# A two-layer decoder step: layer 0's prompt attention laid between its sample batches, with key transposes moved to VectorE

## The reference

```python
# layer 0, per sample request: 8 FoX heads of 64 and 4 differential heads of 2x64, one cache row of 1024 floats
k_all = concatenate([cache_k[pt].reshape(past, 1024), k_b]); v_all likewise; c = cumsum(logf)
sa = q . k * scale + (cq - ck)                  # FoX: causal softmax, then . v
pb = softmax(q . k * scale); diff = pb[0] - lam * pb[1]
ob = rms_norm(diff . v, subln0) * (1 - LAMBDA_INIT)
# layer 0, prompt: the same over the 512 prompt tokens, in blocks of 128 queries
# layer 1: an indexer picks the top 256 keys of each query; 16 query heads over 4 kv heads,
# rows of 256 floats; softmax over the picked keys alone
# after each attention: y += out @ w_out; y += swiglu(rms_norm(y))
```

## Time and profile before

| | us |
|---|---|
| median of 3 runs | 2245.13 |
| lowest, highest | 2235.11, 2249.7 |
| the profiled execution | 2245.45 |
| its span, first to last instruction | 2243.7 |
| TensorE busy | 1873.8 (84%) |
| VectorE busy | 989.5 (44%) |
| ScalarE busy | 569.3 (25%) |
| mean granted TensorE clock | 0.900 |

### The profile page before, as it was taken

How to read it: one execution, slowest core, us unless ns; L and a number is a source line. 1 busy time by engine, 2 the same in 40 slices (tenths; PEclk the granted TensorE clock), 3 DMA queues, 4 the chain that set the end, 5 groups by cost and what they waited for, 6 DMA issues and landing times. The chain is left out here.

```text
span 2243.7 us, 30894 instructions
## 1 busy us (share of the span) xinstructions
PE 1873.8 (84%) x11782; PEld 1460.6 (65%) x11790; DVE 989.5 (44%) x1686; ACT 569.3 (25%) x1051; POOL 138.0 (6%) x111
## 2 busy tenths in 40 slices
PE   3997678488878999999979768566688899999998
PEld 2765445255556997799767543243445699879986
DVE  3436357644433322232234657999343423132312
ACT  2312135233322321122222222233122322112210
POOL 0423002000000000000001320000000000000000
PEclk9998879799988999999999865688788899999999
DMA  4231100499822231223213300000354222223221
GB/s 151 71 103 47 53 10 1 144 381 344 317 79 66 75 94 66 75 81 88 66 52 114 80 0 4 7 1 1 102 153 113 66 75 75 71 79 86 75 71 57
DMA packets 176270, 201.57 MB, mean 90 GB/s; under 512 B 21290, under 2 KB 130666, under 8 KB 176170
## 3 DMA queue, kind: packets, MB, share of 16 engines
q1 hardware_dynamic: 169176, 193.55, 27.3%
q10 hardware_dynamic: 6914, 6.45, 0.9%
q0 software_dynamic: 80, 0.26, 0.0%
HBM read 191.01 MB, written 9.22 MB: 89 GB/s over the span
## 5 line engine op out<-in xcount | busy, mean ns | idle before, releaser
L206 PE MATMUL ps<-feat_lo,w_hi 128*128 128x288 f32 (+1 forms) x1424 | 422.2, 297 | 15.3 <-PEq L436 8.6
L188 DVE TENSOR_TENSOR w_lo<-w_raw,w_hi 128x2048 fp32r<-128x2048 f32 x97 | 222.4, 2293 | 466.4 <-ACT w_hi L182 466.4
L208 PE MATMUL ps<-feat_hi,w_hi 128*128 128x288 f32 (+1 forms) x1424 | 422.3, 297 | 0.0
L207 PE MATMUL ps<-feat_hi,w_lo 128*128 128x288 f32 (+1 forms) x1424 | 421.9, 296 | 0.0
L182 ACT ACTIVATE w_hi<-w_raw 128x2048 fp32r<-128x2048 f32 x97 | 185.5, 1913 | 448.8 <-PE ps L208 415.4
L206 PEld LDWEIGHTS ps<-feat_lo,w_hi 128*128 128x128 f32 (+1 forms) x1424 | 267.5, 188 | 18.3 <-issue 9.1
L208 PEld LDWEIGHTS ps<-feat_hi,w_hi 128*128 128x128 f32 (+1 forms) x1424 | 267.3, 188 | 1.2
L207 PEld LDWEIGHTS ps<-feat_hi,w_lo 128*128 128x128 f32 (+1 forms) x1424 | 267.4, 188 | 1.1
L206 PE MATMUL ps<-w_lo,feat_hi 128*128 128x512 f32 (+2 forms) x560 | 228.5, 408 | 12.6 <-DVE feat_lo L1439 9.5
L207 PE MATMUL ps<-w_hi,feat_lo 128*128 128x512 f32 (+2 forms) x560 | 223.9, 400 | 0.0
L208 PE MATMUL ps<-w_hi,feat_hi 128*128 128x512 f32 (+2 forms) x560 | 222.9, 398 | 0.0
(11 more groups left out here) (236 smaller groups left out, 2299.1 us busy)
## 6 DMA issues: line engine op xcount, KB each, us to landing
s_kslot<-in_cache_l_k_dram SPq DMA_DIRECT2D x64, 512.0 KB, 7.9
s_vslot<-in_cache_l_v_dram SPq DMA_DIRECT2D x64, 512.0 KB, 7.4
w_raw<-in_w_gate_dram SPq DMA_DIRECT2D x44, 512.0 KB, 4.0
w_raw<-in_w_up_dram SPq DMA_DIRECT2D x44, 512.0 KB, 5.2
w_raw<-in_w_in_dram SPq DMA_DIRECT2D x18, 1024.0 KB, 5.2
w_raw<-in_w_down_dram SPq DMA_DIRECT2D x16, 1024.0 KB, 5.1
s_kslot<-in_cache_l_k_dram SPq DMA_DIRECT2D x64, 128.0 KB, 2.2
s_vslot<-in_cache_l_v_dram SPq DMA_DIRECT2D x64, 128.0 KB, 2.7
```

The costliest lines, as they stand in the source:

```text
L188: dve.tensor_tensor(self.K.w_lo[:, n % 2, :], self.K.w_raw[:, n % 2, :], self.K.w_hi[:, n % 2, :].bitcast(F32), ALU.subtract).then_inc(sel ...
L206: pe.matmul(out, lhs[0], rhs[1], start=start, stop=False)
L207: pe.matmul(out, lhs[1], rhs[0], start=False, stop=False)
L208: return pe.matmul(out, lhs[0], rhs[0], start=False, stop=stop)
```

## The change

Layer 0: `prompt_attention` becomes the class `PromptAttention`, a list of steps each of which can be issued alone, and it uses banks 0 to 3 only: one pair of score banks, one bank T for transposes, one for outputs. `sample_attention` becomes `SampleAttention` on banks 4 to 7. `attend` issues both in one block: for each sample request, scores, two prompt steps, transposed weights, one step, weighting, one step, the output's transpose, and what is left of this request's share of the 36 steps (4 or 5 each). The prompt's pairs run with the mixed ones first. The prompt sub-norm is done per pair: ScalarE squares, a product with a column of ones per tile, a power -0.5 on GpSimd, a transpose of the spread factors. The GpSimd scaling of mixed units is folded into the blend.

Keys of the sample requests are turned by VectorE in 32x32 blocks, so that TensorE and the copies out of PSUM have no part in it. That leaves the keys split in four groups g (key 128 j + 32 g + i of page j lies in partition group g, column 32 j + i), and the queries are laid out block-diagonally over the four groups (`qz`, filled by GpSimd), so that one product of 256 columns scores all 1024 keys of a head: row 32 c + 8 g + q, column 32 j + i. Four rounds t of four heads each fill the scores. The maximum of a query is taken over its four groups by a 32x32 transpose, and the sums are folded by a small product. The bias rows and the values are laid out to match: values of page j go to partitions 32 (j % 4) to 32 (j % 4) + 31, four rows to a partition. Layer 0's key pages have a ring of four slots over `resid`, which is loaded again from the input at the end of the block; values lie over `w_hi` and `w_lo`.

Layer 1 uses the same classes: `prompt_alone` issues the prompt's steps with the top-k steps between them, then `attend` runs the sample requests without a prompt. Its mask is stored in 32 rearranged pieces and one for the new tokens.

The diff, cut to its core:

```diff
+class PromptAttention:
+
+
+    BANKS = 4
...
+        self.probs, self.probs_t = sb("probs", [P, 2, 2, SEQ]), sb("probs_t", [P, 2, 2, SEQ])
+        self.minus, self.total = sb("minus", [P, 2 * n]), sb("total", [P, 2 * n])
+        self.ratio, self.norm = sb("ratio", [P, 2]), sb("norm", [P, 2, 8])
+        self.bank = [K.ps[:, i, :] for i in range(2)]
+        self.both, self.T, self.O = K.ps[:, 0:2, :], K.ps[:, 2, :], K.ps[:, 3, :]
...
+        def scores(u):
+            _, p, qt = self.units[u]
+            w, diag = self.width(u), slice(qt * P, (qt + 1) * P)
+            if u >= 1:
+                pe.wait_ge(S["exped"], 2 * u)
+            for i in range(2):
+                pe.matmul(self.bank[i][:, 0:w], self.q_at(p, i, qt), self.k_at(p, i)[:, 0:w], start=True, stop=False)
+            for i in range(2):
+                out = self.bank[i]
+                if self.gates and not self.mixed(p):
+                    pe.matmul(out[:, 0:w], K.c_sel[:, 2 * p + i, :], K.c_rows[:, 0:w], start=False, stop=False)
+                if self.mask is None:
+                    ins = pe.matmul(out[:, diag], K.ident_bf[:, :], K.causal_bf[:, :], start=False, stop=True)
+                else:
+                    ins = pe.matmul(out[:, 0:w], K.ident_bf[:, :], self.mask[:, qt, 0:w], start=False, stop=True)
+            ins.then_inc(S["scored"], 1)
+
+        def turn(u):
+            _, p, qt = self.units[u]
+            for i in self.heads_of(u):
+                if self.mixed(p):
+                    pe.wait_ge(S["blended"], self.n_mixed[u + 1])
+                else:
+                    pe.wait_ge(S["exped"], 2 * u + 1 + i)
+                self.bank_free(pe, ("turn", u, i))
+                for j in range(qt + 1):
+                    ins = pe.transpose(self.T[:, j * P:(j + 1) * P], self.probs[:, u % 2, i, j * P:(j + 1) * P],
+                                       K.c("ident"))
+                ins.then_inc(S["turned"], 1)
...
+    def scalar(self, act, x):
+        S, K, n = self.S, self.K, self.n
+        if 1 <= x <= n:
+            u = x - 1
+            for i in self.heads_of(u):
+                self.bank_filled(act, ("turn", u, i))
+                if u >= 2:
+                    act.wait_ge(S["weighed"], u - 1)
+                act.activation(self.probs_t[:, u % 2, i, 0:self.width(u)], self.T[:, 0:self.width(u)], ACT.Copy)\
+                   .then_inc(S["t_free"], 1)
+        if x < n:
+            act.wait_ge(S["shifted"], x + 1)
+            if x >= 2:
+                self.bank_filled(act, ("turn", x - 2, self.heads_of(x - 2)[-1]))
+            for i in range(2):
+                act.activation(self.probs[:, x % 2, i, 0:self.width(x)], self.bank[i][:, 0:self.width(x)], ACT.Exp,
+                               bias=self.minus[:, 2 * x + i:2 * x + i + 1],
+                               accum_out=self.total[:, 2 * x + i:2 * x + i + 1]).then_inc(S["exped"], 1)
...
+        if 1 <= x <= n and self.mixed(self.units[x - 1][1]):
+            u = x - 1
+            first, second = self.total[:, 2 * u:2 * u + 1], self.total[:, 2 * u + 1:2 * u + 2]
+            dve.wait_ge(S["exped"], 2 * u + 2)
+            s.ok(dve.reciprocal(self.ratio[:, 0:1], second))
+            s.wait()
+            s.ok(dve.scalar_tensor_tensor(out=self.ratio[:, 1:2], in0=self.ratio[:, 0:1], scalar=K.minus_lam[:, 0:1],
+                                          in1=first, op0=ALU.mult, op1=ALU.mult))
+            s.wait()
+            keys = [self.probs[:, u % 2, i, 0:self.width(u)] for i in range(2)]
+            dve.scalar_tensor_tensor(out=keys[0], in0=keys[1], scalar=self.ratio[:, 1:2], in1=keys[0],
+                                     op0=ALU.mult, op1=ALU.add).then_inc(S["blended"], 1)
+        if x < n:
+            dve.wait_ge(S["scored"], x + 1)
+            dve.tensor_reduce(self.minus[:, 2 * x:2 * x + 2], self.both[:, :, 0:self.width(x)], AX, ALU.max, negate=True)\
+               .then_inc(S["shifted"], 1)
...
+    def load_k(self, sp, b, pages):
+        S = self.S
+        for j in pages:
+            n = b * N_PAGES + j
+            if j == self.QUAD:
+                if b >= 1:
+                    sp.wait_ge(S["scored"], 3 * b)
+                sp.dma_start(self.bias[:, :], self.row_bias(b)).then_inc(S["bias_in"], 16)
+                if self.new_bias is None:
+                    sp.dma_start(self.bias_new[:, :], self.K.mask_new[b]).then_inc(S["bias_in"], 16)
+            if n >= self.ring:
+                sp.wait_ge(S["k_turned"], n - self.ring + 1)
+            page = sp.value_load(self.K.pages[0:1, n:n + 1], min_val=0, max_val=self.cache_k.shape[0] - 1)
+            sp.dma_start(self.kslot[:, n % self.ring, :], self.cache_k[ds(page, 1), :, :].rearrange("a k d -> (a k) d"))\
+              .then_inc(self.k_in[n % self.ring], 16)
+
+    def load_v(self, sp, b, pages):
+        S = self.S
+        for j in pages:
+            n = b * N_PAGES + j
+            if j == 0:
+                if b >= 1:
+                    sp.wait_ge(S["weighed"], b)
+                sp.dma_start(self.vnew[:, :], self.new_v(b)).then_inc(S["new_v_in"], 16)
+            page = sp.value_load(self.K.pages[0:1, n:n + 1], min_val=0, max_val=self.cache_v.shape[0] - 1)
+            src = self.cache_v[ds(page, 1), :, :].rearrange("a (g i) d -> (a i) g d", g=4)
+            sp.dma_start(self.vslot[self.rows4[j % self.QUAD], j // self.QUAD, :, :], src).then_inc(self.v_in[j], 16)
+
+    def scores(self, pe, b):
...
+        for t in range(4):
+            if biased(t):
+                at = t * 256 if self.bias.shape[1] > 256 else 0
+                pe.matmul(self.SC[:, t, :], self.bias_sel, self.bias[:, at:at + 256], start=True, stop=True)
+            for e in range(2):
+                for i in range(4):
+                    ins = pe.matmul(self.SC[self.rows4[i], t, :], self.qz[:, 2 * (4 * t + i) + e, :],
+                                    self.keys_at(4 * t + i, e)[1], start=(e == 0 and not biased(t)), stop=True,
+                                    skip_group_check=True)
+            if t % 2:
+                ins.then_inc(S["scored"], 1)
+        if b >= 1:
+            pe.wait_ge(S["o_copied"], b)
+        for t in range(4):
+            if biased(t):
+                row = self.bias_new[:, :] if self.new_bias is None else self.new_bias[:, t, b * DEC_SEQ:(b + 1) * DEC_SEQ]
+                pe.matmul(self.NEWS[:, t, :], self.new_sel, row, start=True, stop=True)
+            for e in range(2):
+                for i in range(4):
+                    new = self.new_k[self.rows4[b // 4], self.keys_at(4 * t + i, e)[0], b % 4 * DEC_SEQ:(b % 4 + 1) * DEC_SEQ]
+                    ins = pe.matmul(self.NEWS[self.rows4[i], t, :], self.qz[own, 2 * (4 * t + i) + e, :], new,
+                                    start=(e == 0 and not biased(t)), stop=True, skip_group_check=True)
+        ins.then_inc(S["scored"], 1)
...
+    def weigh(self, pe, b):
+        S = self.S
+        if b >= 1:
+            pe.wait_ge(S["o_copied"], b)
+        pe.wait_ge(S["pt_out"], 2 * b + 2)
+        pe.wait_ge(S["ptn_ok"], b + 1)
+        for a in range(2):
+            for j in range(self.QUAD * a, self.QUAD * (a + 1)):
+                pe.wait_ge(self.v_in[j], b * 16 + 16)
+            for g in range(4):
+                for t in range(4):
+                    pe.matmul(self.O[self.rows4[t], :], self.pt[:, 2 * t + a, g, :], self.vslot[:, a, g, self.values[t]],
+                              start=(a == 0 and g == 0), stop=False)
+        pe.wait_ge(S["new_v_in"], b * 16 + 16)
+        for t in range(4):
+            ins = pe.matmul(self.O[self.rows4[t], :], self.ptn[:, t, :], self.vnew[:, self.values[t]],
+                            start=False, stop=True)
+        ins.then_inc(S["weighed"], 1)
...
+    def probs_out(self, act, b):
+        S = self.S
+        for half in range(2):
+            act.wait_ge(S["pt_turned"], 3 * b + 1 + half)
+            if b >= 1:
+                act.wait_ge(S["weighed"], b)
+            for x in range(4):
+                ins = act.activation(self.pt[:, 4 * half + x, :, :].rearrange("p g (c q) -> p g c q", c=4),
+                                     self.PT[half][:, x * P:(x + 1) * P].rearrange("p (c g q) -> p g c q", c=4, g=4),
+                                     ACT.Copy)
+            ins.then_inc(S["pt_out"], 1)
...
+    def turn_k(self, dve, b, pages):
+        S = self.S
+        each = self.blocks // len(self.kt)
+        for j in pages:
+            n = b * N_PAGES + j
+            dve.wait_ge(self.k_in[n % self.ring], 16 * (n // self.ring + 1))
+            for x, kt in enumerate(self.kt):
+                if b >= 1:
+                    dve.wait_ge(S["scored"], 3 * b - 1 if x == len(self.kt) - 1 else 3 * b - 2)
+                src = self.kslot[:, n % self.ring, 32 * each * x:32 * each * (x + 1)]
+                ins = dve.transpose(kt[:, :, 32 * j:32 * j + 32], src.rearrange("p (c i) -> p c i", i=32))
```

(82 more changed lines are left out.)

## The result

The changed kernel takes 2415.64 us (median of 4 runs, 2405.81 to 2421.7), the kernel before 2240.68 on the same chip (4 runs): 1.076 times, 95% interval 1.0725 to 1.0789. The forecast was about 2275 us, with 2335 as the upper end of its range. The profiled execution has a span of 2419.9 us, 176.2 more than before.

The account below looks back on a forecast made before the run. Layer 0's sample batches were taken as near two bounds, DMA loads and TensorE, and layer 1's prompt as bound by VectorE. Terms -32 + 0 + 10 + 52 = +30 on 2245.45 us gave about 2275, range 2195 to 2335.

Parts of the forecast that it names:

- Direction: Whole kernel: slower, +30 us on 2245.45; chance of slower 0.45, within 1% 0.25, faster by over 1% 0.30.
- With the low clock for part of it 20.5: Layer 1's sample batches: one chain of 18.9 us, 20.5 with some low clock, against 13.5 before; +52 us (+35 to +75).
- 4.5 us at full clock, 5.0 at 0.80: Layer 1's prompt, per plain unit: single banks' chain replaces VectorE's 5.0 us; 0 us in all, -10 to +15.
- VectorE's bound: Layer 1's prompt before: VectorE busy 152.2 of 162.0 us; would lose the 0.93 us reciprocal and some 0.8 of copies per unit.
- The mask's store, 0.35 us each: Behind layer 1's prompt: 33 transfers instead of one, 11.5 us, formerly hidden; with top-k in draining steps, +10 us.
- 33 to 36 us per batch: Layer 0's sample batches with prompt steps between: path at full clock, above 29.6 us of DMA; layer 0 -32 us.
- scores at 311: Layer 0's start: after first keys and values, sums end near 303; four more pages and transposes lead to scores at 311.
- rival 2: Layer 0: VectorE's block transpose takes twice the copy's time, 1.38 us; +70, 2330 us; chance 0.12.
- 16 us of TensorE work on the path: Layer 0, each batch: part of the path that a lower clock stretches; at 0.87, +18 us for the stage.
- the 220 GB/s assumed: Layer 0's value loads into 32 partitions, at the half-width loads' rate: 19.1 of 29.6 us DMA per batch.
- Rival 1: Faster: layer 0's overlap nearly complete, DMA loop paces it, 257 us instead of 296; 2215 or 2195 us; chance 0.28.
- Rival 3: The layers cancel: layer 0 gains 55 to 60 us and layer 1 loses as much; 2245 us; chance 0.17.

Follow-up runs that it names:

- run 4: Changed kernel with extra identity products of 256 columns put into TensorE's gaps in layer 1's requests, 88 products more; 2361.94 us.
- Runs 5 and 9: Changed kernel, layer 1's prompt: first with a second pair of score banks, 2432.8 us; then also a second bank for turned weights, 2387.48 us.
- run 13: Kernel before, with layer 1's prompt attention from the changed kernel, two score pairs and two turned banks, mask stored in one transfer; 2232.11 us, 0.9946 times before.
- runs 8 and 15: Changed kernel with four, then ten, added identity products of 128 columns in some of layer 0's prompt steps; 2414.72 and 2421.84 us.
- run 6: Changed kernel with layer 0's value pages loaded over all 128 partitions, so the requests' outputs are not the reference's; 2407.4 us.

## Why the prediction was wrong

- **Direction** was right: the shared code costs layer 1 more than layer 0 can give. Layer 0's gain did not come at all, and layer 1's losses were too small.
- **"With the low clock for part of it 20.5"**, with the range of 18 to 23 us, for layer 1's requests: this is the step that failed most, 62 of the 146 us by which the forecast was off. The chain itself was priced well: at a clock of 0.94 the requests are 20.2 us apart (run 4; its added products may lie partly on the path), against 18.9 summed at full clock. But the forecast took a little off the full clock, where the trace has 0.56 for the stage. It had read the 0.83 of the earlier trace rows as a property of the stage. In that stage TensorE did the next request's key transposes in its waits, and the change moves just these to VectorE. Run 4 shows that filling such waits brings the clock back; that the transposes were what held it before is the reading that fits, but they were not put back by themselves.
- **"4.5 us at full clock, 5.0 at 0.80", 0 us for layer 1's prompt**: the chain was named rightly, the term was mis-sized. It took 5.7 us a unit (183.8 / 32), 24 us more in all. The other 12 of the stretch's +36 us are that the mask is now ready at the end of the stage and not 12.7 us ahead of it, which the forecast knew and had in its next term. By the nine profiles the stage would be some 170 us at the clock of 0.80 that the forecast took, an estimate a little beyond their range: so about 13 of the 24 us are the lower clock again, 0.69, and the rest is the chain. Runs 5 and 9 show that with two of each bank, and not with two score pairs alone, the stage is 26 us shorter at an equal clock. That VectorE's bound would vanish was right, and run 13 shows what it was worth.
- **The mask's store, 0.35 us each**: 0.71 measured, 22.75 us for 32. As a stretch it came out at +7.8 against +10 all the same, because the drain of the prompt that used to follow the mask now lies ahead of it.
- **Layer 0, "33 to 36 us per batch"**, 36 with its share of the clock: 44.4 us. The start (scores at 311) and VectorE's transposes were right, so rival 2 (twice the copy's time) was not it; its own sum, 2275 + 70, is 2345 and not 2330. Three terms look too small, the last by measurement. The printed terms add up to 32 to 35 us with mixed steps but to 36 to 39 with plain ones, some 36 in the mean, where the sum took 34. The clock was 0.73, not 0.87: by the forecast's own 16 us of TensorE work on the path that is another 3.5 us a request, an estimate that runs 8 and 15 neither bear out nor refute. The value pages at less than the 220 GB/s assumed make 1.2 of it (run 6). That is 6 to 7 of the 8.4 us; the rest is open.
- **Rival 1** (a nearly complete overlap, paced by the transfers) was far off: with the requests alone the transfers set 34.6 us, not 29.6, and interleaved a request takes 10 more. **Rival 3** would have needed a gain in layer 0, which there was not.

Layer 0's single banks were not doubled: with requests beside the prompt all eight banks are in use.

## What to carry to other kernels

Work that fills TensorE's waits may be what keeps its clock: before moving it away, price the stage that stays at the lower level, and look at the granted clock of a stage together with what fills its gaps. To learn what a low clock costs, compare profiles in which the same code ran at different clocks; filling gaps tells it only where the filling doesn't lie on the path. When banks are taken from two to one, write out the whole round trip through each, for giving back one of two single banks can give nothing. Share code between two stages only after both have been priced: here the half that was meant to gain cost 16 us, and the half that merely shared the code 155.

## What the runs showed of the hardware

- In nine profiles with the same code in layer 1's prompt, the granted clock was 0.63 to 0.77 and the stage 190 to 173 us long, with VectorE and ScalarE busy for the same time.
- TensorE's granted clock went from 0.56 to 0.94 in layer 1's requests when idle gaps were filled with useless products; the same score group took 1.94 us at one level and 1.07 at the other, and the kernel became 54 us faster by doing more.
- Value pages of 512 KB into 32 partitions held the transfers at 247 GB/s for keys and values together, at a share of 0.97; over 128 partitions the same bytes moved at 285 GB/s and a share of 0.77.
- A block transpose of 128x512 on VectorE took 0.66 us, no more than the copy of that shape out of PSUM.
- A store with rows cut into pieces of 128 bytes held SP's queue for 0.71 us; a store of all rows whole, 0.48.
